# Order of units in the feed-forward layers of a two-block transformer kernel: both down units ahead of P4, T4 later, T1 later in one layer

## Chip, core and metric

One NeuronCore of a Trainium2 chip runs the whole kernel in one launch. The metric is the device time of one execution in microseconds (us). TensorE multiplies; ScalarE (ACT) and VectorE (DVE) prepare its operands and take its results; GpSimd (POOL) issues accumulating transfers and computes small statistics; SyncE (SP) issues most loads. All data is float32.

## What is computed

The input is 256 tokens of width 1024. A first block applies a forgetting attention with a pooling branch, a cross attention over a memory and a gated feed-forward layer; a second block has two layers with two gated feed-forward layers each, a short gated convolution in the first and a differential attention in the second. So there are five feed-forward layers, and most of the time is theirs. In short form:

```
gu  = rmsnorm(h) @ w_gate_up            # 1024 -> 2 * 2816
act = silu(gu[:, :2816]) * gu[:, 2816:]
h   = h + act @ w_down                  # 2816 -> 1024
```

In the second block the result is normalised and halved before it is added. The change touches only the order of work inside these five layers.

## The kernel before

**Precision.** A float32 matrix X is used as two float32r parts, hi = round(X) by ScalarE and lo = X - hi by VectorE, and each product is three matmuls (hi by lo, lo by hi, hi by hi; lines 2115 to 2117, for the down projection 2571 to 2573). So for every unit of weights, a 128x2048 tile, ScalarE writes `w_hi` (line 769 from a loaded tile `w_raw`, line 1084 from a block or a sum of blocks) and then VectorE writes `w_lo` (line 1366), and TensorE waits for `w_lo`. There are three slots for the parts; ScalarE may write unit u once TensorE has used unit u-3 in the order of the list `FFN_OPS`.

**The products.** The up projection of a layer f (0 to 4; "first" to "fifth") has 11 column groups of 256. Groups N0, N1 and N2 are multiplied plainly. The other eight form four pairs p = 0 to 3 (in the texts the number in brackets, P5(1), is the pair). A pair is a 2x2 problem of weight blocks (B11, B12, B21, B22) and token halves, done with seven products P1 to P7 in place of eight. P1, P2 and P3 use B11, B21 and B22; the others use sums: T1 (from B11 and B12) for P5, T2 (T1 and B22) for P6, T3 (B12 and B22) for P7 and T4 (T2 and B21) for P4. VectorE computes T1, T2 and T4 with `weight_sum` (line 1385, whole 128x2048 tiles); T1 goes to the tile `KT`, T2 to `VD`, and T4 takes T2's place in `VD`. T3 is made in B12's own place (`Z`) by an accumulating DMA that POOL issues once T1 has been summed (line 601), and for pairs 1 and 2 T4 is made by such a DMA too, once P6's low part is written. So VectorE sums T4 only for pairs 0 and 3. Each product is 12 matmuls of 128x512.

**Results and activations.** ScalarE copies P1, P5 and P6 out of PSUM (`keep`, line 1115), VectorE combines them with later products to C22, C12 and C11 (`result`, lines 1805, 1807, 1809), ScalarE applies silu (`square_gate`, line 1101), VectorE multiplies by the up half (`square_act`, line 1817), TensorE transposes (line 2595), and the transposed activations are split by `act_out` on ScalarE (`act_hi`, line 1121) and VectorE (`act_lo`, line 1823).

**The down projection** has 11 units of 256 rows, 24 matmuls each: D0 and D1 (of N0 and N1), then two for each pair (Da, Db) and DN2. The pair's two units run in the pair behind: Da(p-1) and Db(p-1) with pair p.

**Order.** Every engine executes its own list in order, and the lists are written out by hand; semaphores count the units. `FFN_OPS` gives the order of units, from which the counts of `w_hi`, `w_lo` and `w_used` and the slots follow. In a layer TensorE runs N0, N1, P1(0), P2(0), P5(0), P6(0), P3(0), P7(0), D0, P4(0), D1, and then for each pair P1, P5, P6, the transposes of the activations, P3, P7, Da, P2, P4, Db. The lists of the other engines are the two functions `ffn` of the scalar part (from line 1125) and the vector part (from line 1823), and `ffn` of the sync part for the loads. A load of the next pair's block waits until the block of this pair has been split (`next_block`); B21 of pair 1 also waits until T4(0) has been summed, as that sum reads B21. D1's activations go into the same tiles as D0's, so `act_out(1)` waits until D0 has been used.

Of the kernel before, what the change touches and what calls it, by code (L numbers as in the profile page):

```python
# [53 lines left out]
SQUARES = 4  # L54
GROUPS = SQUARES + 3
FFN_OPS = [("N0a", 0), ("N0b", 0), ("N1a", 0), ("N1b", 0)]
FFN_OPS += [(_n, 0) for _n in ("P1", "P2", "P5", "P6", "P3", "P7")] + [("D0", 0), ("P4", 0), ("D1", 0)]
for _p in range(1, SQUARES):
    FFN_OPS += [("P1", _p), ("P5", _p), ("P6", _p), ("P3", _p), ("P7", _p), ("Da", _p - 1), ("P2", _p), ("P4", _p),
                ("Db", _p - 1)]  # L60
# [97 lines left out]
def build(nc, a, out):  # L158
# [5 lines left out]
    with ctx:  # L164
# [28 lines left out]

        def act_parts(d):

            return (ahi1, alo1) if is_second(d) else (ahi, alo)

        work = sb("work", [P, 4096])
        junk = sb("junk", [P, HALF])
# [205 lines left out]
        def _(sp):  # L405
# [22 lines left out]
            def ffn(f, w_gu, w_dn, first_blocks=None, next_gu=None):  # L428

                u0 = U_FFN[f]  # L430
                gu = w_gu.rearrange("(k p) f -> p k f", p=P)

                def up(name):
                    u = u0 + OP[name, 0]
                    j = {"N0": 0, "N1": 1, "N2": FJ - 1}[name[:2]]
                    k0 = 4 * (name[-1] == "b")
                    r = raw[raw_slot(u)][:, :].rearrange("p (k c) -> p k c", k=4)
                    load(u, [(r[:, :, 0:256], gu[:, k0:k0 + 4, j * 256:j * 256 + 256]),
                             (r[:, :, 256:512], gu[:, k0:k0 + 4, j * 256 + FF:j * 256 + FF + 256])])

                def down(name, p=0):
                    u, d = u0 + OP[name, p], down_block(name, p)
                    rows = w_dn[d * 256:d * 256 + 256, :].rearrange("(k p) f -> p k f", p=P)
                    load(u, [(raw[raw_slot(u)][:, D * k:D * k + D], rows[:, k, :]) for k in range(2)])

                def next_block(name, reader, p):

                    if p + 1 < SQUARES or next_gu is not None:
                        sp.wait_ge(w_lo, u0 + OP[reader, p] - 1)
                        if name == "B21" and p == 0:  # L450
                            sp.wait_ge(t_ok, sums_ready(f, 0, "T4"))
                        block_in(name, (p + 1) % SQUARES, w_gu if p + 1 < SQUARES else next_gu)

                def first_block(name):
                    if first_blocks:
                        block_in(name, 0, w_gu)

                up("N0a")
                up("N0b")
                up("N1a")  # L460
                if f == 4:
                    for w in first_blocks:
                        sp.wait_ge(*w)
                    first_block("B11")
                up("N1b")
                if f in (0, 2):
                    for w in first_blocks:
                        sp.wait_ge(*w)
                    first_block("B11")
                first_block("B12")  # L470
                first_block("B21")
                first_block("B22")
                down("D0")
                down("D1")
                down("Da", 0)
                next_block("B11", "P1", 0)
                next_block("B22", "P3", 0)
                next_block("B21", "P2", 0)
                next_block("B12", "P7", 0)
                down("Db", 0)  # L480
                down("Da", 1)
                for p in range(1, SQUARES):
                    next_block("B11", "P1", p)
                    next_block("B22", "P3", p)
                    next_block("B12", "P7", p)
                    if p == 1:
                        down("Db", 1)
                        next_block("B21", "P2", p)
                        down("Da", 2)
                    elif p == 2:  # L490
                        down("Db", 2)
                        next_block("B21", "P2", p)
                        up("N2a")
                    else:
                        up("N2b")
                        next_block("B21", "P2", p)
                        down("Da", 3)
                        down("Db", 3)
                        down("DN2")
# [253 lines left out]
        def _(act):  # L753
# [297 lines left out]
            def ffn(f, stat, reader, gain, k0=0, kv=False):  # L1051
# [64 lines left out]

                def act_out(d):
                    act.wait_ge(act_t, FJ * f + d + 1)
                    if d == 1:
                        act.wait_ge(w_used, u0 + OP["D0", 0] + 1)  # L1120
                    act.activation(act_parts(d)[0][:, :], act_bank(d)[:, :], ACT.Copy).then_inc(act_hi, 1)

                weights("N1b")
# [15 lines left out]
                keep("P1", 0)  # L1139
                block("P6", 0)  # L1140
                block("P3", 0)
                keep("P5", 0)
                block("P7", 0)
                keep("P6", 0)
                weights("D0")
                block("P4", 0)
                weights("D1")
                act_out(1)
                for p in range(1, SQUARES):
                    block("P1", p)  # L1150
                    square_gate(p - 1, 0)
# [202 lines left out]
        def _(dve):  # L1354
# [405 lines left out]
            def ffn(f, stat, reader, gain, update=lambda t: None, kv=False):  # L1760
# [78 lines left out]
                block("P5", 0)  # L1839
                block("P6", 0)  # L1840
                block("P3", 0)
                weight_sum("T4", f, 0)
                block("P7", 0)
                weights("D0")
                block("P4", 0)
                result("C22", 0)
                weights("D1")
                result("C12", 0)
                weight_sum("T1", f, 1)
                act_out(1)  # L1850
                result("C11", 0)
                for p in range(1, SQUARES):
                    block("P1", p)
                    weight_sum("T2", f, p)
                    block("P5", p)
                    square_act(p - 1, 0)
                    square_act(p - 1, 1)
                    block("P6", p)
                    if p not in ADDED_T4:
                        weight_sum("T4", f, p)  # L1860
                    block("P3", p)
                    block("P7", p)
                    act_out(2 * p)
                    weights("Da", p - 1)
                    act_out(2 * p + 1)
                    block("P2", p)
                    result("C22", p)
                    block("P4", p)
                    result("C12", p)
                    if p + 1 < SQUARES:  # L1870
                        weight_sum("T1", f, p + 1)
                    weights("Db", p - 1)
                    result("C11", p)
                weights("N2a")
                square_act(SQUARES - 1, 0)
                weights("N2b")
# [224 lines left out]
        def _(pe):  # L2101
# [433 lines left out]
            def ffn(f, reader, waits, kv=False, turned=False, nxt=None):  # L2535
# [72 lines left out]
                for p in range(SQUARES):  # L2608
# [18 lines left out]
                        block("P2", p)  # L2627
                    else:
                        down("D0")
                    pe.wait_ge(c_ok, m + 1)  # L2630
                    block("P4", p)
                    if p:
                        down("Db", p - 1)
                    else:
                        down("D1")
                pe.wait_ge(c_ok, 3 * SQUARES * (f + 1))
                up_unit("N2a")
                turn_act(2 * SQUARES, 1 + SQUARES)
# [314 lines left out]
```

## Time and profile before

| | |
|---|---|
| median of 3 runs | 1264.8 us (1263.88 to 1267.02) |
| profiled execution, its own time | 1265.15 us |
| its span, first to last instruction | 1263.4 us |
| mean granted TensorE clock | 0.999 of full speed |
| TensorE busy / weight loads busy | 1249.7 / 1029.2 us |
| VectorE busy | 1042.2 us (82%) |
| ScalarE busy | 804.7 us (64%) |
| GpSimd busy | 197.8 us (16%) |
| read from HBM | 275.24 MB, 219 GB/s over the span |

Busy time is the time in which an engine executes; the share is of the span. TensorE's matmuls are pipelined: a 128x512 matmul is recorded with some 0.39 us, and the next starts 0.23 us after it, so a wait is best read from one start to the next. An instruction's "idle before" is the time in which its engine executed nothing, and the arrow names what ended it. A few matmul records are missing from the trace.

### The profile page before, as it was taken

Reading aid. Unit: us, or ns where it says so; the run is one execution under the profiler, and the core shown is the slowest. Engines: PE = TensorE matmul, PEld = TensorE weight load, DVE = VectorE, ACT = ScalarE, POOL = GpSimd, SP = SyncE. Lnnn points to the kernel's source line nnn. Section 1 sums busy time; section 2 is a strip of 40 time slices with the busy share of each in tenths; the row PEclk is TensorE's granted clock in tenths of the full one; section 3 lists DMA queues with packets and bytes.
Section 4 is the critical chain, followed back from the end, with each engine's and each line's share of the span. In section 5 each row is a group of like instructions: output and inputs, shape, how many; then the busy total and the mean of one; then the engine's idle time right before and its main releaser. Section 6 shows DMA issues by size and latency. Waiting matters only on the chain.

```text
span 1263.4 us, 15541 instructions
## 1 busy us (share of the span) xinstructions
PE 1249.7 (99%) x5897; PEld 1029.2 (81%) x5897; DVE 1042.2 (82%) x1036; ACT 804.7 (64%) x988; POOL 197.8 (16%) x224
## 2 busy tenths in 40 slices
PE   9999999999999999999999999999999999999998
PEld 7888888888888888888878888888888877788886
DVE  6766689999799996767899997999977568899984
ACT  6674576666576664645666664766656467766662
POOL 6142130110001100202301101211001003301100
PEclk9999999999999999999999999999999999999999
DMA  9537498997649955568989978389745535999931
GB/s 335 175 101 229 128 327 251 267 273 250 199 147 253 272 172 187 194 223 213 334 242 247 265 248 260 123 240 274 219 167 179 180 125 170 321 287 263 266 133 44
DMA packets 143003, 277.32 MB, mean 220 GB/s; under 512 B 8993, under 2 KB 39897, under 8 KB 142929
## 3 DMA queue, kind: packets, MB, share of 16 engines
q1 hardware_dynamic: 120192, 229.67, 52.1%
q0 software_dynamic: 22288, 45.54, 19.7%
q8 instruction: 47, 0.77, 0.2%
q10 hardware_dynamic: 448, 1.12, 0.2%
q14 instruction: 28, 0.22, 0.1%
HBM read 275.24 MB, written 1.05 MB: 219 GB/s over the span
## 4 chain that ended last, share of the span: by engine, by line
PE 83%; DVE 8%; DMA 3%; issue 3%; ACT 2%; POOL 0%; SPq 0%; DVEq 0%; POOLq 0%; ACTq 0%
PE B L2115 15%; PE B L2117 15%; PE B L2116 15%; PE B L2571 7%; PE B L2573 7%; PE B L2572 7%; DVE w_lo L1366 5%; PE T L2115 3%; PE T L2117 3%; PE T L2116 3%; DMA Z<-in_ffn_w_gu 2%; DVE VD L1385 1%; ACT w_hi L1084 1%; PE T L2595 1%; DMA VD<-in_ffn_w_gu 1%
## 5 line engine op out<-in xcount | busy, mean ns | idle before, releaser
L1366 DVE TENSOR_TENSOR w_lo<-w_raw,w_hi 128x2048 fp32r<-128x2048 f32 x129 | 296.5, 2300 | 87.3 <-ACT w_hi L769 87.0
L769 ACT ACTIVATE w_hi<-w_raw 128x2048 fp32r<-128x2048 f32 x129 | 247.2, 1919 | 102.2 <-PE B L2573 59.7
L2115 PE MATMUL B<-w_hi,xt_lo 128*128 128x512 f32 x652 | 259.8, 398 | 2.4 <-DVE nat L2029 0.6
L2117 PE MATMUL B<-w_hi,xt_hi 128*128 128x512 f32 x652 | 254.5, 390 | 0.0
L2116 PE MATMUL B<-w_lo,xt_hi 128*128 128x512 f32 x652 | 254.1, 390 | 0.0
L2571 PE MATMUL B<-w_hi,act_lo 128*128 128x512 f32 x440 | 172.8, 393 | 0.8 <-DVE w_lo L1366 0.6
L2573 PE MATMUL B<-w_hi,act_hi 128*128 128x512 f32 x440 | 171.5, 390 | 0.0
L2572 PE MATMUL B<-w_lo,act_hi 128*128 128x512 f32 x440 | 171.3, 389 | 0.0
L2115 PEld LDWEIGHTS B<-w_hi,xt_lo 128*128 128x128 f32 x652 | 122.5, 188 | 31.5 <-issue 4.4
L2117 PEld LDWEIGHTS B<-w_hi,xt_hi 128*128 128x128 f32 x652 | 122.4, 188 | 26.1
L2116 PEld LDWEIGHTS B<-w_lo,xt_hi 128*128 128x128 f32 x652 | 122.6, 188 | 23.3
L2115 PE MATMUL B<-w_hi,mem_T_lo 128*128 128x512 f32 x296 | 118.6, 401 | 0.9 <-DVE w_lo L1366 0.9
L2117 PE MATMUL B<-w_hi,mem_T_hi 128*128 128x512 f32 x296 | 115.6, 391 | 0.0
L2116 PE MATMUL B<-w_lo,mem_T_hi 128*128 128x512 f32 x296 | 115.4, 390 | 0.0
L1084 ACT ACTIVATE w_hi<-VD 128x2048 fp32r<-128x2048 f32 x40 | 76.8, 1920 | 55.9 <-PE B L2573 34.8
L2571 PEld LDWEIGHTS B<-w_hi,act_lo 128*128 128x128 f32 x440 | 82.6, 188 | 19.7 <-DVE w_lo L1366 2.0
L2573 PEld LDWEIGHTS B<-w_hi,act_hi 128*128 128x128 f32 x440 | 82.6, 188 | 17.4
L2572 PEld LDWEIGHTS B<-w_lo,act_hi 128*128 128x128 f32 x440 | 82.6, 188 | 16.6
L1366 DVE TENSOR_TENSOR w_lo<-Z,w_hi 128x2048 fp32r<-128x2048 f32 x40 | 91.4, 2286 | 4.3 <-ACT w_hi L1084 4.3
L1366 DVE TENSOR_TENSOR w_lo<-VD,w_hi 128x2048 fp32r<-128x2048 f32 x40 | 91.5, 2287 | 2.2 <-ACT w_hi L1084 2.1
L601 POOL DMA_DIRECT2D Z<-in_ffn_w_gu x32 | 39.0, 1449 | 331.9 <-DVE KT L1385 331.9
L1084 ACT ACTIVATE w_hi<-Z 128x2048 fp32r<-128x2048 f32 x40 | 76.5, 1913 | 9.3 <-PE B L2117 5.1
(331 smaller groups left out, 2115.9 us busy)
## 6 DMA issues: line engine op xcount, KB each, us to landing
w_raw<-in_ffn_w_down SPq DMA_DIRECT2D x88, 512.0 KB, 5.8
Z<-in_ffn_w_gu SPq DMA_DIRECT2D x64, 512.0 KB, 8.2
w_raw<-in_ffn_w_gu SPq DMA_DIRECT2D x48, 512.0 KB, 5.3
nat<-in_ffn_w_gu SPq DMA_DIRECT2D x32, 512.0 KB, 7.9
QT<-in_ffn_w_gu SPq DMA_DIRECT2D x32, 512.0 KB, 7.0
Z<-in_ffn_w_gu POOLq DMA_DIRECT2D x32, 512.0 KB, 9.1
w_raw<-in_conv_w_in SPq DMA_DIRECT2D x24, 512.0 KB, 4.8
w_raw<-in_w_down SPq DMA_DIRECT2D x22, 512.0 KB, 6.6
```

The costliest lines, as they stand in the source:

```text
L601: pool.dma_start(r[:, i:i + 2, :], gu[:, 4 + i:6 + i, col:col + HALF], accum_op=ALU.add)\
L769: act.activation(whi[home(u)][:, :], raw[slot][:, :], ACT.Copy).then_inc(w_hi, 1)
L1084: act.activation(whi[home(u)][:, :], (WB[src] if src in WB else WT[src]), ACT.Copy).then_inc(w_hi, 1)
L1366: dve.tensor_tensor(wlo[home(u)][:, :], src, whi[home(u)][:, :].bitcast(F32), ALU.subtract).then_inc(w_lo, 1)
L1385: dve.tensor_tensor(WT[name], src, WB[block_name], ALU.add).then_inc(t_ok, 1)
L2115: pe.matmul(bank[:, :], lo[:, k, x], whi[s][:, c], start=first, stop=False, skip_group_check=more)
L2116: pe.matmul(bank[:, :], hi[:, k, x], wlo[s][:, c], start=False, stop=False, skip_group_check=more)
L2117: return pe.matmul(bank[:, :], hi[:, k, x], whi[s][:, c], start=False, stop=last, skip_group_check=more)
L2571: pe.matmul(o, lo[:, x], whi[slot][:, c], start=d == 0 and k == 0, stop=False)
L2572: pe.matmul(o, hi[:, x], wlo[slot][:, c], start=False, stop=False)
L2573: ins = pe.matmul(o, hi[:, x], whi[slot][:, c], start=False, stop=d == FJ - 1 and k == 1)
L2595: ins = pe.transpose(act_bank(d)[:, (2 * k + t) * P:(2 * k + t) * P + P], actn[:, t, c0 + k * P:c0 + k * P + P], ident[:, :])
```

## The change

1. *First pair of every layer.* The order of units becomes P7, D0, D1, P4 in place of P7, D0, P4, D1, on TensorE and in `FFN_OPS`. D1's activations get the second pair of tiles (`ahi1`, `alo1`), so `act_out(1)` no longer waits for D0; it moves to just behind P3's unit on ScalarE and on VectorE. ScalarE splits D1 ahead of P4. On VectorE T4(0) moves from ahead of P7's low part to behind D0's, P4's low part to behind C12, and C11 comes ahead of T1(1). SP issues the load of B12 ahead of that of B21.
2. *Fourth pair of every layer.* On VectorE T4(3) moves from ahead of P3's low part to behind the second `act_out` of the pair, ahead of P2's.
3. *Third layer only (f == 2), pairs 1 and 2.* On VectorE T1 of the next pair moves from ahead of Db's low part to behind Db's low part and C11.

```diff
-FFN_OPS += [(_n, 0) for _n in ("P1", "P2", "P5", "P6", "P3", "P7")] + [("D0", 0), ("P4", 0), ("D1", 0)]
+FFN_OPS += [(_n, 0) for _n in ("P1", "P2", "P5", "P6", "P3", "P7", "D0", "D1", "P4")]
...
         def act_parts(d):
-            return (ahi1, alo1) if is_second(d) else (ahi, alo)
+            return (ahi1, alo1) if d == 1 or is_second(d) else (ahi, alo)
...
                 next_block("B11", "P1", 0)
                 next_block("B22", "P3", 0)
+                next_block("B12", "P7", 0)
                 next_block("B21", "P2", 0)
-                next_block("B12", "P7", 0)
...
                 def act_out(d):
                     act.wait_ge(act_t, FJ * f + d + 1)
-                    if d == 1:
-                        act.wait_ge(w_used, u0 + OP["D0", 0] + 1)
...
                 block("P3", 0)
+                act_out(1)
                 keep("P5", 0)
                 block("P7", 0)
                 keep("P6", 0)
                 weights("D0")
+                weights("D1")
                 block("P4", 0)
-                weights("D1")
-                act_out(1)
...
                 block("P3", 0)
-                weight_sum("T4", f, 0)
+                act_out(1)
                 block("P7", 0)
                 weights("D0")
-                block("P4", 0)
+                weight_sum("T4", f, 0)
                 result("C22", 0)
                 weights("D1")
                 result("C12", 0)
+                block("P4", 0)
+                result("C11", 0)
                 weight_sum("T1", f, 1)
-                act_out(1)
-                result("C11", 0)
                 for p in range(1, SQUARES):
...
                     block("P6", p)
-                    if p not in ADDED_T4:
-                        weight_sum("T4", f, p)
                     block("P3", p)
                     block("P7", p)
                     act_out(2 * p)
                     weights("Da", p - 1)
                     act_out(2 * p + 1)
+                    if p not in ADDED_T4:
+                        weight_sum("T4", f, p)
                     block("P2", p)
                     result("C22", p)
                     block("P4", p)
                     result("C12", p)
-                    if p + 1 < SQUARES:
+                    if p + 1 < SQUARES and f != 2:
                         weight_sum("T1", f, p + 1)
                     weights("Db", p - 1)
                     result("C11", p)
+                    if p + 1 < SQUARES and f == 2:
+                        weight_sum("T1", f, p + 1)
...
                     else:
                         down("D0")
+                        down("D1")
                     pe.wait_ge(c_ok, m + 1)
                     block("P4", p)
                     if p:
                         down("Db", p - 1)
-                    else:
-                        down("D1")
```

## Rows read from the trace of the kernel before

**Rows 1.** The page: the span, and busy us, share and instructions of TensorE.
```profile
span 1263.4 us, 15541 instructions
...
PE 1249.7 (99%) x5897; PEld 1029.2 (81%) x5897; DVE 1042.2 (82%) x1036; ACT 804.7 (64%) x988; POOL 197.8 (16%) x224
```

**Rows 2.** Busy time by stretch: stretch, us long, busy us by engine, clock, DMA share, GB/s.
```profile
core 0: us, PE busy (x) PEld busy (x) DVE busy (x) ACT busy (x) POOL busy (x), PEclk, DMA share, GB/s
...
206.00:214.00 8.00, 8.00 (x37) 6.57 (x36) 7.92 (x7) 3.99 (x5) 2.07 (x2) 1.00 0.89 324
```

**Rows 3.** Timeline of TensorE, first layer, last matmul of P3(0) and first of P7(0).
```profile
200.85 0.39 PE L2117 MATMUL B<-w_hi,mem_T_hi 128*128 128x512 f32 x1
201.52 0.47 PE L2115 MATMUL T<-w_hi,mem_T_lo 128*128 128x512 f32 x1 [0.28 <-DVE w_lo L1366]
```

**Rows 4.** List of waits, whole span: us in total, times, longest.
```profile
PE T L2115 <- DVE w_lo L1366: 1.3, 5, 0.3
...
PE B L2571 <- DVE act_lo L1823: 0.2, 1, 0.2
...
DVE KT L1385 <- DMA Z<-in_ffn_w_gu: 1.8, 4, 0.6
```

**Rows 5.** Timeline of VectorE, first layer: T4(0), P7, act_lo(1), P5(1), P6(1).
```profile
196.88 2.29 DVE L1385 TENSOR_TENSOR VD<-VD,QT 128x2048 f32<-128x2048 f32 x1
199.09 2.28 DVE L1366 TENSOR_TENSOR w_lo<-Z,w_hi 128x2048 fp32r<-128x2048 f32 x1
...
211.55 0.68 DVE L1823 TENSOR_TENSOR act_lo<-T,act_hi 128x512 fp32r<-128x512 f32 x1
...
217.15 2.29 DVE L1366 TENSOR_TENSOR w_lo<-KT,w_hi 128x2048 fp32r<-128x2048 f32 x1
...
220.68 2.29 DVE L1366 TENSOR_TENSOR w_lo<-VD,w_hi 128x2048 fp32r<-128x2048 f32 x1
```

**Rows 6.** Timeline of ScalarE, first layer: copy of P5(0), high parts of P7(0), D0.
```profile
195.84 0.60 ACT L1115 ACTIVATE work<-B 128x512 f32<-128x512 f32 x1 [1.20 <-PE B L2117]
196.33 1.91 ACT L1084 ACTIVATE w_hi<-Z 128x2048 fp32r<-128x2048 f32 x1
...
199.05 1.91 ACT L769 ACTIVATE w_hi<-w_raw 128x2048 fp32r<-128x2048 f32 x1
```

**Rows 7.** Timeline of TensorE, first layer: first matmuls of P1(1) and P5(1).
```profile
217.94 0.39 PE L2115 MATMUL B<-w_hi,xt_lo 128*128 128x512 f32 x1
...
220.66 0.39 PE L2115 MATMUL B<-w_hi,mem_T_lo 128*128 128x512 f32 x1
```

**Rows 8.** Timeline of TensorE: transposes to P3(2), P3(3) of layer 1, P3(3) of layer 2.
```profile
256.92 0.60 PE L2595 MATMUL T<-ident,work 128*128 128x128 f32 x4
...
257.71 0.48 PE L2115 MATMUL T<-w_hi,mem_T_lo 128*128 128x512 f32 x1
...
287.73 0.60 PE L2595 MATMUL T<-ident,work 128*128 128x128 f32 x4
...
288.70 0.47 PE L2115 MATMUL B<-w_hi,mem_T_lo 128*128 128x512 f32 x1
...
464.47 0.60 PE L2595 MATMUL T<-ident,work 128*128 128x128 f32 x4
...
465.94 0.47 PE L2115 MATMUL B<-w_hi,mem_T_lo 128*128 128x512 f32 x1 [0.44 <-DVE w_lo L1366]
```

**Rows 9.** Timeline of TensorE, third layer: last matmul of P4(2), first of Db(1).
```profile
721.88 0.39 PE L2117 MATMUL B<-w_hi,xt_hi 128*128 128x512 f32 x1
722.85 0.50 PE L2571 MATMUL B<-w_hi,act_lo 128*128 128x512 f32 x1 [0.58 <-DVE w_lo L1366]
```

**Rows 10.** Timeline of VectorE, third layer: T1(2).
```profile
686.62 2.29 DVE L1385 TENSOR_TENSOR KT<-Z 128x2048 f32<-128x2048 f32 x1 [0.25 <-DMA Z<-in_ffn_w_gu]
```

**Rows 11.** Timeline of ScalarE, third layer: high part of Db(0).
```profile
685.91 1.92 ACT L769 ACTIVATE w_hi<-w_raw 128x2048 fp32r<-128x2048 f32 x1 [2.48 <-PE B L2573]
```

**Rows 12.** Line 601's transfers: T3(1) of the first layer, then T3(2) of the third.
```profile
DMA to landing us min/median/max: 6.0/8.3/10.6
...
DMA to landing us min/median/max: 6.2/9.1/12.0
```

## Prediction

> **What bounds the kernel now.** I read the page first, for the busy share [rows 1]. TensorE is busy 1249.7 of 1263.4 us, so nothing that leaves its work alone can give back much; the change touches no matmul. Then the busy time by stretch: behind the first pair of a layer, from 206 to 214 us, VectorE is busy 7.92 of 8.00 us beside a full TensorE [rows 2]. Two engines are full there, and whoever is late has no room to catch up. So I went to TensorE's timeline and took start to start, since recorded ends overlap the next start. A 128x512 matmul follows the last after 0.23 us; every larger step between two products is a stall. The first matmul of P7 in the first layer starts 201.52 after 200.85, 0.67 us, so 0.44 lost, and it takes 0.47 instead of 0.39, as the first one behind a wait does: 0.08 more [rows 3]. What releases it is VectorE's low part of P7. In the list of waits it stands five times, once a layer [rows 4]: 1.3 us of idle time, plus the 0.16 of overlapped matmul tail each, is 2.1 us. That is what the first edit aims at.
>
> **The first pair, taken away.** VectorE starts the next instruction 0.08 us before the recorded end of the last, so 2048 columns cost 2.20 and 512 columns 0.60 (the 0.68 of act_lo less 0.08) [rows 5]. T4 now sits between P3's low part and P7's. Taken out, P7's low part no longer waits for VectorE but for ScalarE's high part, 196.33+1.91=198.24 [rows 6], and ends at 200.55 instead of 201.37. TensorE could use it at 201.08. The five waits go: 0.44+0.08 in this layer, about 0.5 in each. D1 can follow D0, since its activations are split before P5's copy, in ScalarE's 1.20 us of idle time at 195.84 [rows 6]; with that D1's wait for act_lo in the third layer (0.2 idle and 0.16 of tail [rows 4]) goes too.
>
> **The first pair, given back.** VectorE is the queue to follow. Between the start of T4 (196.88) and that of P5(1)'s low part (217.15) lie 20.27 us [rows 5]: eight large instructions and four small ones (8x2.20+4x0.60=20.0) and 0.27 idle. The change keeps all twelve but opens two gaps that T4 filled: act_lo(1) is done at 197.48 and P7's high part at 198.24, so 0.78 idle; then P7's low part is done at 200.47 and D0's high part only at 199.05+1.91=200.96, so 0.51 idle. ScalarE can't be earlier: its slots come free by TensorE's P5 and P6. P5(1)'s low part therefore starts at 196.88+20.0+1.3=218.2, ends at 220.47, and is usable 0.15 later (201.37 against 201.52 [rows 3, 5]) at 220.6. TensorE, 0.5 earlier than its 220.66 [rows 7], asks at 220.2: it waits 0.45. P6(1)'s low part follows 3.53 us after P5's (217.15 to 220.68, one low part and two gated products [rows 5]), but P5 keeps TensorE only 2.72+0.08 (217.94 to 220.66 for such a block [rows 7]): it waits a further 0.73. Once P5 waits, P6 always waits 0.73. With 0.08 for the first matmul after each, the first layer loses 0.45+0.73+0.16-0.52, some 0.85 us net. Fourth and fifth have the same pattern: 0.85 each. In the second a small wait before a later D unit shrinks by the same shift: 0.65. In the third D1's 0.4 and its 0.08 go too: 0.35, if VectorE follows as in the first (it now waits 0.6 us there for B12, one of four such waits [rows 4], and no longer does). Sum of the first edit: **+3.55**.
>
> The queues it is moved past: T1(1) is 2.2 us later, so POOL's accumulating transfer T3(1) is too (10.6 us from its second issue, 0.7 behind the first, to landing in this layer, so about 225.5 [rows 12]); P7(1)'s high part waits for that to 225.6, low part done 229.8, TensorE asks at 230.5. No cost, 0.6 us in hand. On SP the load of B12 goes ahead by 0.8, and B21 waits for T4, 205.5 instead of 199.3, with Db(0) and Da(1) queued behind it 3 us and none late: they are read after 232. P4's own low part is done at 211.1, asked at 214.7. Free, as long as the loads take what they take now.
>
> **T4(3) behind P3.** In the fourth pair TensorE issues eight transposes and then P3. Where nothing is late that takes 257.71-256.92=0.79 us; with T4(3) ahead 0.97 in the first layer and 1.47 in the second [rows 8]. So 0.18 in three layers and 0.68 in two (the third is like the second): **-1.9**. Its new place is in front of P2, whose low part has 3 us in hand. Free.
>
> **T1 behind D's second unit, third layer.** There Db(1) waits 722.85-721.88-0.23=0.74 [rows 9], and 0.1 goes at its first matmul and 0.1 at Db(0): 0.95 gained. The cost: VectorE is free at 686.37, 0.25 ahead of T1's 686.62 [rows 10], and now has Db(0)'s low part next, whose high part ends at 685.91+1.92=687.83 [rows 11]. It idles 1.49 where it idled 0.25, T1's slot, so P1, T2, P5 and P6 come 1.24 later. By the arithmetic above: P5(2) waits about 0.37 and P6(2) 0.73, and again in the next pair. T1(2) itself ends 4 us later (692.9), and POOL's transfer queues behind it: its second half lands 12.0 us after its issue [rows 12], at 705.9; P7(2)'s high and low parts take 1.92+2.30 and it is usable at 710.3, asked at 709.4: 0.84, and Da behind it 0.47 and 0.38. Sum 3.9, with 0.08 at six first matmuls 4.4, less 0.95: +3.4. The unknown is the landing, as the transfer now meets other loads. No row shows it there. If it lands 0.5 us sooner the edit costs 2.4 and 1 us sooner 1.6; 1 us later, 5.4. The span of its kind is 10.6 to 12.0 [rows 12]; I take the upper end less a little: **+3.0**.
>
> **Sum.** 3.55-1.9+3.0=+4.65 us. The profiled execution took 1265.15 us (span 1263.4), 0.35 above the median of 1264.8; the sum gives 1269.8 on the first and 1269.45 on the second. I say 1269.5.
>
> **A rule to weigh.** The rows show where TensorE has its gaps: at P7, at P3 and at the D units [rows 3, 4, 8, 9], 5.8 us in all. The Trainium skill, "Perfetto Trace Analysis", section Identifying Performance Opportunities, says to take the engine with the highest occupancy, find its gaps and make what ends them come sooner. By that rule alone this change is a gain, and it is the first rival; the sum above differs because VectorE, which ends those gaps, is itself full [rows 2].
>
> **Rivals.**
> *All the waits go and none come* (7%). VectorE would have to reach P5(1) 0.45 and P6(1) 1.2 us sooner than my sum; its place is the pair of gaps of 0.78 and 0.51. For it: P5(1) is now ready at 219.44, 1.2 us ahead of its use [rows 5, 7], more than either gap. Against: the two gaps together are 1.3 and TensorE asks 0.5 sooner. All that is removed is 2.1+0.4 (first matmuls)+0.4+1.9+1.0=5.8: 1259.0. It decides where the two gaps together fall under 0.86 us for P5(1) (219.59 is usable now with 0.27 idle, 220.18 is asked) and under 0.1 for P6(1).
> *Only the first pairs lose* (24%). POOL's transfer in the third layer lands a microsecond or more sooner, or the loads leave VectorE ready earlier, and the third edit costs 0 to 1.5: 3.55-1.9+0.7=+2.3, 1267. For it: the load that T1 waited for is long in by then.
> *Transfers collide* (13%). B21, Db(0), Da(1) now follow one another from 205.5 and the additions start later, in stretches where the DMA engines are busy 0.89 of the time [rows 2]; each microsecond later puts waits at P7 and P4. With landings 1 us later the second layer loses 1.4 and the third 2 more: +8, 1273. The Trainium skill, "DMA: Bandwidth & Descriptors", section Issuing engines are not separate DMA queues, says that transfers of every issuing engine interleave on the same 16 engines; by it POOL's additions slow whenever SP's bunch up, and this rival is where it would show.
> That the change moves nothing has no room: the orders are written by hand and TensorE's follows them.
>
> **Numbers.** Forecast 56% (+2.8 to +7), the rivals 24, 13 and 7. A measurement of this kernel can tell 0.3% (3.8 us) from no change. Faster by more: only nearly all of the first rival, 0.03. Within: the second rival, the rest of the first and the low end of the forecast, 0.33. Slower: 0.64. The range leaves out the first rival and the far end of the third: 1265 to 1273.5.
>
> **What would show it.** Right: in each layer TensorE has no wait at P7(0), and waits near 0.4 at P5(1) and 0.7 at P6(1) for VectorE's low part; VectorE idle 0.8 and 0.5 ahead of P7's and D0's low parts; transposes to P3(3) in 0.8; in the third layer no wait at Db, but at P5, P6 of both later pairs and at P7(2) behind POOL's transfer. Wrong: no wait at P5(1), or the third layer not longer than the first.

## The result, and the profile after

The changed kernel takes 1276.96 us (1276.61 to 1278.67, 4 runs), the kernel before 1264.86 beside it: 1.0093 times as long, 95% interval 1.0081 to 1.0105. That is 12.1 us more where 4.65 were forecast, and beyond the range of 1265 to 1273.5. The profiled execution took 1278.67 us. Its page, to be set against [rows 1] (the third line is the chain of work that ended last, where TensorE's share was 83%, VectorE's 8 and the DMA's 3):

```profile
span 1276.8 us, 15536 instructions
PE 1254.8 (98%) x5897; PEld 1027.9 (81%) x5897; DVE 1042.7 (82%) x1036; ACT 805.1 (63%) x988; POOL 198.4 (16%) x224
PE 66%; DVE 12%; DMA 9%; issue 7%; ACT 4%; POOL 1%; DVEq 0%; SPq 0%; POOLq 0%; ACTq 0%
```

The work is the same on every engine. TensorE's busy time is 5 us up, mostly because the recorded tail of a matmul ahead of a wait is no longer overlapped. What is new is DMA on the chain: 9%. The list of waits, TensorE's alone, of after (us in total, times, longest):

```profile
PE B L2115 <- DVE w_lo L1364: 5.9, 13, 0.6
PE B L2571 <- DVE w_lo L1364: 4.3, 9, 1.2
PE T L2115 <- DVE w_lo L1364: 1.1, 2, 0.6
```

The five waits at P7(0) [rows 4] are gone. Of the fifteen waits at line 2115, one, at 51 us, has nothing to do with the change and is in both kernels; fourteen at the square products stand where before had seven (the five of 1.3 us at P7(0) and two at P3(3)). Ahead of the down units (line 2571) there are nine where it had one of 0.6 us. Where they lie, TensorE's timeline of the first layer tells:

```profile
201.24 0.39 PE L2117 MATMUL B<-w_hi,mem_T_hi 128*128 128x512 f32 x1
201.46 0.39 PE L2115 MATMUL T<-w_hi,mem_T_lo 128*128 128x512 f32 x1
...
220.28 0.39 PE L2117 MATMUL B<-w_hi,xt_hi 128*128 128x512 f32 x1
221.02 0.47 PE L2115 MATMUL B<-w_hi,mem_T_lo 128*128 128x512 f32 x1 [0.36 <-DVE w_lo L1364]
...
223.64 0.39 PE L2117 MATMUL B<-w_hi,mem_T_hi 128*128 128x512 f32 x1
224.55 0.47 PE L2115 MATMUL B<-w_hi,mem_T_lo 128*128 128x512 f32 x1 [0.52 <-DVE w_lo L1364]
...
244.38 0.39 PE L2117 MATMUL B<-w_hi,xt_hi 128*128 128x512 f32 x1
245.43 0.50 PE L2571 MATMUL B<-w_hi,act_lo 128*128 128x512 f32 x1 [0.67 <-DVE w_lo L1364]
```

P7(0) follows P3(0) in 0.22 us, where [rows 3] had 0.67. P5(1) waits 221.02-220.28-0.23=0.51 and P6(1) 0.68: forecast were 0.45 and 0.73. Then Db(0) waits 0.82, and that was not in the forecast. By layer, Db(0) waits 0.83, 1.37, 0, 0.51 and 1.10 us, Db(1) 0.36, 0.53, 0, 0, 0.33, and Da(0) 0.2 to 0.35 in the last four. The way back from the third wait, Db(0)'s, is in VectorE's timeline (answers to [rows 5]):

```profile
198.66 2.29 DVE L1364 TENSOR_TENSOR w_lo<-Z,w_hi 128x2048 fp32r<-128x2048 f32 x1 [0.71 <-ACT w_hi L1084]
201.38 2.29 DVE L1364 TENSOR_TENSOR w_lo<-w_raw,w_hi 128x2048 fp32r<-128x2048 f32 x1 [0.42 <-ACT w_hi L769]
...
222.12 2.28 DVE L1364 TENSOR_TENSOR w_lo<-VD,w_hi 128x2048 fp32r<-128x2048 f32 x1
224.32 2.28 DVE L1364 TENSOR_TENSOR w_lo<-nat,w_hi 128x2048 fp32r<-128x2048 f32 x1
...
238.09 2.29 DVE L1364 TENSOR_TENSOR w_lo<-VD,w_hi 128x2048 fp32r<-128x2048 f32 x1 [1.14 <-ACT w_hi L1084]
...
243.09 2.29 DVE L1364 TENSOR_TENSOR w_lo<-w_raw,w_hi 128x2048 fp32r<-128x2048 f32 x1
```

The two gaps ahead of P7's and D0's low parts, 0.71 and 0.42, are the forecast 0.78 and 0.51. Db(0)'s low part ends at 245.38; it is late because P4(1)'s low part could only start at 238.09. ScalarE's timeline (answers to [rows 6]) says why. P4(1)'s high part waits for a transfer:

```profile
236.14 1.92 ACT L1084 ACTIVATE w_hi<-VD 128x2048 fp32r<-128x2048 f32 x1 [2.99 <-DMA VD<-in_w_gate_up]
```

So the chain to Db(0) begins at POOL's accumulating transfer of T4(1). POOL's issue and SP's next one, of before and then of after:

```profile
223.27 2.38 POOL L601 DMA_DIRECT2D VD<-in_w_gate_up  x2 [8.96 <-DVE w_lo L1366]
225.68 0.96 SPq L426 DMA_DIRECT2D nat<-in_w_gate_up  x2
DMA to landing us min/median/max: 6.2/7.8/9.4
```

```profile
224.70 2.38 POOL L601 DMA_DIRECT2D VD<-in_w_gate_up  x2 [7.76 <-DVE w_lo L1364]
226.63 1.14 SPq L426 DMA_DIRECT2D nat<-in_w_gate_up  x2
DMA to landing us min/median/max: 6.0/8.3/10.7
```

The addition goes out in two halves (x2), 0.7 us between their starts; the landing rows give the shorter and the longer time of the two, each from its own issue. The first lands in about 6 us in both (the minimum). The second lands in 9.4 before and 10.7 after; in the second and third layers it is over 2 us later. And SP's load of B22 (the tile `nat`) comes 2.41 us behind POOL's first issue before, 1.93 after. That offset became the question of the experiments.

How little room there was stands in the trace of before, in rows that the prediction did not use: ScalarE's P4(1) high part, VectorE's low part of Db(0) and TensorE's Db(0) in the first layer, then the last two in the second.

```profile
233.39 1.92 ACT L1084 ACTIVATE w_hi<-VD 128x2048 fp32r<-128x2048 f32 x1 [1.50 <-DMA VD<-in_w_gate_up]
...
240.35 2.28 DVE L1366 TENSOR_TENSOR w_lo<-w_raw,w_hi 128x2048 fp32r<-128x2048 f32 x1
...
243.31 0.39 PE L2571 MATMUL B<-w_hi,act_lo 128*128 128x512 f32 x1
...
417.29 2.28 DVE L1366 TENSOR_TENSOR w_lo<-w_raw,w_hi 128x2048 fp32r<-128x2048 f32 x1
...
419.63 0.50 PE L2571 MATMUL B<-w_hi,act_lo 128*128 128x512 f32 x1
```

Db(0) had 0.68 us in hand in the first layer (242.63 to 243.31), 0.06 in the second and third, 0.72 and 0.73 in the last two.

### The profile page after: what moved, and what is told of

It is laid out like the page before. It is cut to its first block, busy times and chain, and to the rows that moved or that the text cites. A ratio compares the mean times of both kernels' runs of the same rounds, so it can differ in the third digit from the quotient of the medians.

```text
span 1276.8 us, 15536 instructions
## 1 busy us (share of the span) xinstructions
PE 1254.8 (98%) x5897; PEld 1027.9 (81%) x5897; DVE 1042.7 (82%) x1036; ACT 805.1 (63%) x988; POOL 198.4 (16%) x224
## 3 DMA queue, kind: packets, MB, share of 16 engines
HBM read 275.24 MB, written 1.05 MB: 216 GB/s over the span
## 4 chain that ended last, share of the span: by engine, by line
PE 66%; DVE 12%; DMA 9%; issue 7%; ACT 4%; POOL 1%; DVEq 0%; SPq 0%; POOLq 0%; ACTq 0%
PE B L2115 13%; PE B L2117 13%; PE B L2116 13%; DVE w_lo L1364 7%; PE B L2571 5%; PE B L2573 5%; PE B L2572 5%; DMA VD<-in_ffn_w_gu 4%; DMA Z<-in_ffn_w_gu 3%; PE T L2117 2%; PE T L2115 2%; PE T L2116 2%; DVE KT L1383 2%; DMA VD<-in_w_gate_up 2%; ACT w_hi L769 2%
## 5 line engine op out<-in xcount | busy, mean ns | idle before, releaser
L1084 ACT ACTIVATE w_hi<-Z 128x2048 fp32r<-128x2048 f32 x40 | 76.6, 1915 | 31.9 <-DMA Z<-in_ffn_w_gu 11.2
```

What stands on the lines that cost most here:

```text
L1084: act.activation(whi[home(u)][:, :], (WB[src] if src in WB else WT[src]), ACT.Copy).then_inc(w_hi, 1)
```

## The experiments

Medians, with the ratio to the kernel before and its 95% interval. Each edit is against the kernel before unless it says otherwise.

**Each part alone.** The first edit is the hunks of the diff that stand under number 1 of the change; at its core:

```diff
-FFN_OPS += [(_n, 0) for _n in ("P1", "P2", "P5", "P6", "P3", "P7")] + [("D0", 0), ("P4", 0), ("D1", 0)]
+FFN_OPS += [(_n, 0) for _n in ("P1", "P2", "P5", "P6", "P3", "P7", "D0", "D1", "P4")]
```

> The first edit alone (D1 ahead of P4, T4(0) and T1(1) later, B12 ahead of B21), T4(3) and the third layer's T1 as before. Theory 'late addition': T1(1) late makes POOL's transfer T3(1) land some 3 to 7 us later, T4(1) right behind it, and Db(0) waits; this edit holds nearly all of the loss, +12 to +14 us, with TensorE waits near 0.5 at P5(1), 0.7 at P6(1) and 0.5 to 1.4 at Db(0) in each layer. Rival 'sum as predicted': the edit alone is +3.5 and the rest of the loss comes from the other two edits. P3(3)'s step from its transposes stays at 1.0 to 1.5 us, or Db(1) takes the wait.

Measured 1278.02, ratio 1.0106 (1.0092 to 1.0120), some 13.5 us where 3.55 stood in the sum. That is 10 us too little for this part, more than the 7.5 by which the whole sum was short; the parts do not simply add up (below).

The second edit alone:

```diff
                     block("P6", p)
-                    if p not in ADDED_T4:
-                        weight_sum("T4", f, p)
...
                     act_out(2 * p + 1)
+                    if p not in ADDED_T4:
+                        weight_sum("T4", f, p)
```

> Only T4(3) moved from ahead of P3's low part to ahead of P2's. By the predicted sum it gives back 0.18 us in three layers and 0.68 in two, -1.9 us in all (0.15%), and the step from the transposes to P3(3) is 0.8 us in every layer. Rival: T4(3) in its new place makes P2(3) or Db(2) wait, 0 or more.

Measured 1262.48, ratio 0.9984 (0.9975 to 0.9992). TensorE's timeline of the first layer, the transposes of the fourth pair (the first four of eight) and P3(3):

```profile
287.60 0.60 PE L2595 MATMUL T<-ident,work 128*128 128x128 f32 x4
...
288.39 0.48 PE L2115 MATMUL B<-w_hi,mem_T_lo 128*128 128x512 f32 x1
```

0.79 from transposes to P3(3) as forecast, 0.97 in [rows 8], and in the second layer 464.70-463.91=0.79 too.

The third edit alone:

```diff
-                    if p + 1 < SQUARES:
+                    if p + 1 < SQUARES and f != 2:
                         weight_sum("T1", f, p + 1)
                     weights("Db", p - 1)
                     result("C11", p)
+                    if p + 1 < SQUARES and f == 2:
+                        weight_sum("T1", f, p + 1)
```

> Only the third layer's T1(2) and T1(3) moved behind Db's low part and C11. Predicted sum: no wait at Db(0) and Db(1), waits at P5 and P6 of pairs 2 and 3 of 0.4 and 0.7, P7(2) 0 to 0.9 by when POOL's transfer lands; +3.0 us (1.6 to 5.4). Rival 'fill': the load T1 waited for is long in and the third layer is not longer, -0.5 to +1.

Measured 1268.17, ratio 1.0030 (1.0019 to 1.0040): +4.0, forecast +3.0. Its waits in the third layer are at P5(2) and P6(2), where they were forecast (timeline of TensorE), and again at P5(3) and P6(3), 0.89 and 0.71:

```profile
698.43 0.39 PE L2119 MATMUL B<-w_hi,xt_hi 128*128 128x512 f32 x1
699.11 0.47 PE L2117 MATMUL T<-w_hi,mem_T_lo 128*128 128x512 f32 x1 [0.29 <-DVE w_lo L1366]
...
701.70 0.39 PE L2119 MATMUL T<-w_hi,mem_T_hi 128*128 128x512 f32 x1
702.64 0.47 PE L2117 MATMUL B<-w_hi,mem_T_lo 128*128 128x512 f32 x1 [0.55 <-DVE w_lo L1366]
```

The first and second edits together:

> First and second edit, the third layer's T1 as before. If the third edit costs what it costs alone (+3), this is 3 us faster than the changed kernel, near 1274. If in the changed kernel VectorE is late there anyway and Db(0) of the third layer would wait as in the other layers, the third edit is worth about nothing in company and this is 1276 to 1277, with Db(0) waiting 0.8 to 1.6 in the third layer too.

Measured 1275.17, ratio 1.0088 (1.0073 to 1.0104). So in company the third edit costs less than alone, 1.8 us by the medians and 0.6 by the ratios: without it Db(0) of the third layer waits 1.8 us behind T4(1), with it not at all, since VectorE then sums T1(2), 2.2 us, only behind Db(0)'s low part.

**Which piece of the first edit.** First theory: the additions are late because T1(1) ends 2.2 us later. The first edit, with T1(1) behind D1's low part, and a wait so that T2(1) is not written before P4's low part is done:

```diff
+                weight_sum("T1", f, 1)
                 result("C12", 0)
                 block("P4", 0)
                 result("C11", 0)
-                weight_sum("T1", f, 1)
...
+                    if p == 1:
+                        dve.wait_ge(w_lo, u0 + OP["P4", 0] - 1)
                     weight_sum("T2", f, p)
```

> The first edit with one thing changed: VectorE sums T1(1) right behind D1's low part, 3.4 us sooner than in the edit and 1 us sooner than in the kernel before. Theory 'late addition' (T3(1) is issued late and T4(1) cannot land before some 10 us after T3(1) has): T3(1) lands near 222, T4(1) near 235, Db(0) waits 0 to 0.3 us; P5(1) and P6(1) still wait 0.5 and 0.7. So +3 to +6 us against before, 8 to 10 less than the first edit. Rival 'loads' (B21, Db(0) and Da(1) loaded later are what makes the additions slow or Db late): these loads are as in the edit, so Db(0) waits as it did and the time stays near 1278.

Measured 1277.62, ratio 1.0096 (1.0082 to 1.0110). The theory fell: T3(1) landed at 223.3 in place of 226.0 in the first layer, and Db(0) still waited 1.73 us, behind a T4(1) of 12.3 us.

Next, D1 ahead of P4 as in the change, but VectorE's T4(0) ahead of P7's low part and SP's order as before:

```diff
                 block("P3", 0)
                 weight_sum("T4", f, 0)
                 block("P7", 0)
                 weights("D0")
-                block("P4", 0)
+                act_out(1)
                 result("C22", 0)
                 weights("D1")
                 result("C12", 0)
-                weight_sum("T1", f, 1)
-                act_out(1)
+                block("P4", 0)
                 result("C11", 0)
+                weight_sum("T1", f, 1)
```

> D1 ahead of P4 as in the first edit, but T4(0) stays ahead of P7's low part and SP's loads keep their order; T1(1) stays behind C11, 1.4 us later than before. P7(0) waits its 0.44 again. VectorE has no gaps of 0.8 and 0.5, so P5(1) and P6(1) wait 0 to 0.1. Theory 'late addition' splits here: if an addition slows because it is issued late, T3(1) lands some 12 us after its issue and Db(0) waits 0.5 to 1.5 (+3 to +7 us in all); if it slows because of the loads beside it, T3(1) lands after 10 us, T4(1) is not held, Db(0) waits under 0.3 and the time is -1 to +2.

Measured 1267.41, ratio 1.0016 (1.0007 to 1.0026). T3(1) is as slow as in the changed kernel (11.4 to 12.5 us), yet T4(1) takes 10.0 to 10.5 in all layers and Db(0) waits 0.12 at most. So a slow T4(1) does not come from a slow T3(1) ahead of it. The same, with T1(1) behind D1's low part and the same added wait:

```diff
                 weights("D1")
+                weight_sum("T1", f, 1)
                 result("C12", 0)
                 block("P4", 0)
                 result("C11", 0)
-                weight_sum("T1", f, 1)
```

> D1 ahead of P4 on TensorE and ScalarE, T4(0) ahead of P7's low part and T1(1) right behind D1's low part (where it waits for B12's load near 207 to 208.5). If the two late sums are the whole harm of the first edit, this is the kernel before less D1's wait in the third layer: -0.5 us, between -1.5 and +1. If putting D1 ahead of P4 itself costs (slots, P5(1)'s high part behind D1, gates behind P4), +2 or more.

Measured 1269.54, ratio 1.0036 (1.0022 to 1.0050), a miss. This run split by layer. In the first, fourth and fifth T4(1) took 9.9 to 10.2 us and Db(0) did not wait; in the second and third it took 12.3 and 12.5, and Db(0) waited 1.69 and 1.89. One kernel, one order, two durations. The rows of its second layer, POOL's issue and SP's:

```profile
401.62 2.43 POOL L601 DMA_DIRECT2D VD<-in_ffn_w_gu  x2 [11.04 <-DVE w_lo L1364]
403.55 1.19 SPq L426 DMA_DIRECT2D nat<-in_ffn_w_gu  x2
```

1.93 us between the issues in these two layers, 2.12 in the other three. That gave the theory that the next runs test: a load that SP issues before POOL has got its second half out goes in ahead of that half, and it lands some 2 us later.

**The theory, forwards.** The changed kernel, with SP's load of B22 held back until ScalarE has written P7's high part:

```diff
                         sp.wait_ge(w_lo, u0 + OP[reader, p] - 1)
...
+                        if name == "B22" and p in (1, 2):
+                            sp.wait_ge(w_hi, u0 + OP["P7", p] - 1)
```

> The changed kernel, with one thing added: SP issues the loads of B22 for pairs 2 and 3 only when ScalarE has written P7's high part, about 1.3 us later than now. Theory (a load that SP issues before POOL has issued the second half of its accumulating transfer gets in ahead of that half): in every layer T4(1) lands 9.9 to 10.5 us after its first issue instead of 11.4 to 12.7, the waits at Db(0) (0.83, 1.37, 0.51 and 1.10 us over the usual step of 0.23) go, and 4 to 5 us come back: 1272.5. The waits at P5(1), P6(1) and Da(0) stay. Rival (the transfer is slow because it starts late, among more loads): it lands as late as before and the time stays at 1277.

Measured 1271.98, ratio 1.0051 (1.0037 to 1.0065): 5 us back, by delaying a load. T4(1) took 9.1 to 10.1 us in every layer and no Db waits. POOL's and SP's issues of the first layer and the landing, and TensorE at Db(0):

```profile
224.98 2.38 POOL L603 DMA_DIRECT2D VD<-in_w_gate_up  x2 [7.76 <-DVE w_lo L1366]
228.17 0.99 SPq L426 DMA_DIRECT2D nat<-in_w_gate_up  x2
DMA to landing us min/median/max: 6.0/7.6/9.3
```

```profile
244.66 0.39 PE L2119 MATMUL B<-w_hi,xt_hi 128*128 128x512 f32 x1
244.88 0.39 PE L2573 MATMUL B<-w_hi,act_lo 128*128 128x512 f32 x1
```

The load comes 3.19 us behind now, the second half lands in 9.3, and Db(0) follows P4(1) in 0.22.

**And T3's too.** On top of it, SP's load of B11 behind T2:

```diff
+                        if name == "B11" and p:
+                            sp.wait_ge(t_ok, sums_ready(f, p, "T2"))
```

> As the run with B22 later, and SP also issues the load of B11 for the next pair only behind T2 of this one, 2.2 us later than now, so that it follows both halves of T3's transfer. Theory: T3(1) to T3(3) land about 10 us after their issue instead of 11.1 to 12.5, P7(1)'s high part no longer waits for T3(1) (idle 1.33 us in the first layer), the waits at Da(0) of 0.2 to 0.34 go in four layers, and 1 to 2 us more come back: 1271. Rival: landings and time do not move.

Measured 1276.34, ratio 1.0085 (1.0072 to 1.0099): the time missed by 5 us, the landings in part. T3(1) landed 8.4 to 9.0 us after its issue, where it took 11.3 to 12.1 in the run before, and the waits at Da(0) went. But P7(1)'s high part, no longer held by T3(1), now ended so early that waiting for it delayed SP no more. Timeline of POOL and SP, first layer:

```profile
224.36 2.38 POOL L605 DMA_DIRECT2D VD<-in_w_gate_up  x2 [7.76 <-DVE w_lo L1368]
226.28 1.16 SPq L426 DMA_DIRECT2D nat<-in_w_gate_up  x2
```

1.93 us again in all five layers (here by the rounded rows 1.92); T4(1) took 11.6 to 12.4 again and Db(0) waited 0.97 to 1.84 in four of them. It is a second, unplanned test of the offset, and it speaks for it.

**The theory, backwards.** The kernel before, with POOL's transfer a little later, so that SP's load falls inside its two issues (`tick` is a new tile of 8 columns that nothing reads):

```diff
                     pool.wait_ge(w_lo, U_FFN[f] + OP["P6", p] - 1)
+                    if p == 1:
+                        pool.wait_ge(w_hi, U_FFN[f] + OP["P3", p] - 1)
+                        pool.memset(tick[:, :], 0.0)
```

> The kernel before, with the one thing reversed: POOL issues T4(1)'s transfer some 0.4 to 0.5 us later, behind ScalarE's high part of P3(1) and a memset of 8 columns, so that SP's load of B22 comes 1.9 to 2.0 us behind the first issue instead of 2.4. Theory of the load that gets in: the transfer takes 12 us or more instead of 10.1, lands 2.4 us later, and Db(0), whose low part is ready only 0.05 to 0.75 us ahead of TensorE in the kernel before, waits 1.8 us in the first, fourth and fifth layers and 2.4 in the second and third: 1264.9+10=1275. Rival (lateness alone): it lands 0.45 later, Db(0) waits 0.4 in two layers, 1266.

Measured 1275.74, ratio 1.0085 (1.0069 to 1.0100): +10.6, forecast +10. Waits of TensorE, and POOL, SP and TensorE of the first layer:

```profile
PE B L2575 <- DVE w_lo L1370: 8.5, 6, 1.9
```

```profile
223.94 0.10 POOL L603 MEMSET tick<- 128x8 f32 x1 [9.13 <-ACT w_hi L1088]
224.39 2.39 POOL L605 DMA_DIRECT2D VD<-in_w_gate_up  x2 [0.35 <-issue]
226.16 1.32 SPq L427 DMA_DIRECT2D nat<-in_w_gate_up  x2
...
244.98 0.50 PE L2575 MATMUL B<-w_hi,act_lo 128*128 128x512 f32 x1 [1.01 <-DVE w_lo L1370]
```

The offset is 1.77, T4(1) takes 11.3 to 12.5 us and Db(0) waits 1.2 to 2.1 in all layers. The issue itself is 0.65 us later than before (224.39 against 223.27, in an execution that is 0.47 behind at P7(0)). Lateness of 0.65 alone would have put next to nothing on the three layers with 0.68 to 0.73 in hand, and 0.6 on the other two.

All T4(1) transfers, five layers in each of fourteen kernels, sorted by the time from POOL's first issue to SP's next load:

| SP's load behind POOL's first issue | transfers | first issue to landing |
|---|---|---|
| 1.77 to 1.93 us | 32 | 11.27 to 13.20 us |
| 2.12 to 3.93 us | 38 | 9.15 to 10.48 us in 36, 11.3 in 2 |

The two exceptions are in the second layer of the kernels below, at 2.42 and 2.85.

**The queues in the trace.** The packets that start on each DMA queue show what the two transfers do to each other. In the first layer of before queue q0 carries 1.05 MB from POOL's first issue (223.27) to 234, the size of the addition, so q0 is POOL's and q1 has SP's loads. The microsecond from 5.5 to 6.5 us behind POOL's first issue, in before (228.77 to 229.77) and then in after (230.20 to 231.20), as packets, MB, share of the 16 DMA engines:

```profile
q0 software_dynamic: 67, 0.13, 74.0%
q1 hardware_dynamic: 31, 0.06, 23.7%
```

```profile
q1 hardware_dynamic: 182, 0.37, 100.4%
q0 software_dynamic: 3, 0.00, 0.5%
```

Before, the addition goes on beside the load. After, it stops between its halves while SP's load has the engines. In that microsecond q0 starts 0 to 4 KB in all 32 transfers of the first row of the table and 94 to 194 KB in all 38 of the second. In the two exceptions it did not stop: 98% of the transfer had started by 9.2 us, as in the other 36, and the last packets followed one by one, 0.25 us apart.

T4(1) is not alone. Of the other additions in two halves that POOL issues from 200 us on (T3 and the other T4), 313 have a first half that lands within 7 us (51 do not, and are left out). With SP's next load 1.93 us behind or less, all 180 took 11.05 us or more; with it 2.08 or more behind, 116 of 133 took under 10.5 (the others, most of them in the second and third layers, up to 11.7). The trace of before had this already: there T3(1) has the next load 3.1 us behind and takes 10.0 to 10.2 in four layers (11.3 in the first), T3(2) and T3(3) have it 1.93 behind and take 11.2 to 13.6.

**The parts that pay.** The second edit, with D1's activations in their own tiles and ScalarE's `act_out(1)` behind P3, so that the third layer's wait for act_lo goes; the units in the order of before:

```diff
-            return (ahi1, alo1) if is_second(d) else (ahi, alo)
+            return (ahi1, alo1) if d == 1 or is_second(d) else (ahi, alo)
...
                 result("C22", 0)
+                if f == 2:
+                    act_out(1)
                 weights("D1")
                 result("C12", 0)
                 weight_sum("T1", f, 1)
-                act_out(1)
+                if f != 2:
+                    act_out(1)
```

> The kernel before with T4(3) behind P3 (measured -1.7 us) and D1's activations in their own tiles, split ahead of P5's copy on ScalarE; on VectorE act_out(1) stands ahead of D1's low part in the third layer alone. The third layer's D1 no longer waits (0.45 us). Expected -2.1 us against before (-1.3 to -3), the fastest so far. If it is only -1.7 or less, the time saved at D1 is taken by the next wait of that layer, at Db.

Measured 1262.58, ratio 0.9977 (0.9968 to 0.9987): the fastest by ratio (the second edit alone has the lower median, 1262.48, beside other runs of before), ahead of both kernels. The gain of 0.23% is under the 0.3% of the prediction's text, but its interval stays below 1; from the second edit alone it can't be told apart. With both delays of SP's loads on top:

> The kernel with the good parts (T4(3) behind P3, D1's activations in their own tiles), with both delays of SP's loads. Theory: T3(2), T3(3) and both T4 transfers of the second layer land in about 10 us; the two waits at Db in the second layer (0.54 and 0.65) go: 1261.3, 1.2 us under the same kernel without the delays. Rival: 1262.5, as without them.

Measured 1262.84, ratio 0.9981 (0.9973 to 0.9990): no gain, a miss. Its T4(1) were 2.4 us or more ahead of the load already, and the two long transfers of the second layer stayed long (11.3 and 11.6 us, Db waits 0.54 and 1.02), so the offset is not their cause. What made their last packets late stays open.

## Why the prediction was wrong

**What held.** The waits at P7(0) went in all layers. The two gaps, and from them P5(1) and P6(1) by the arithmetic of VectorE's queue: 0.45 and 0.73 forecast, 0.51 and 0.68 to 0.72 measured. T4(3) behind P3: -1.9 forecast, -1.7 measured. T1 in the third layer: +3.0 forecast, +4.0 alone, with waits at the forecast places except P7(2), and one more at P3(3), 740.14 of its timeline, which ScalarE's copy released. Its size came out near by some luck: the 0.84 at P7(2) did not come, and P5(3) waited 0.89 where about 0.4 was forecast.

**What failed** is one step, the queues that the first edit is moved past: "Free, as long as the loads take what they take now." The condition was named, and it did not hold. The step followed T3(1) to P7(1) and stopped. T3(1) landed at 226.0, not 225.5, in the first layer; in the other four it took 11.9 to 12.3 us instead of 10.0 to 10.2, with SP's next load 1.93 us behind its start instead of 3.1, and there Da(0) waits, up to 0.35. T4(1) was not followed in the sum, from its issue by P4(1)'s parts to Db(0). Measured from P7(0), where this execution of after is 0.39 behind that of before apart from the edit (201.24 against 200.85 for the matmul ahead of it), P6(1)'s low part ends 1.05 us later (222.12 against 220.68) and TensorE asks for Db(0) 0.90 later (244.61 against 243.31). So lateness alone takes 0.15 of the slack, which is 0.63 (the 0.68 in hand less the 0.05 from the end of the low part to TensorE's start); the transfer's own 1.3 us more takes the rest and makes the wait: 0.15+1.3-0.63=0.82. In the second layer nothing was in hand; the transfer took 2.6 us longer, and about half of it reached Db(0), a wait of 1.37: VectorE before had waited 0.62 us for another load, ahead of T1(2), and now did not, and TensorE itself lost 0.35 at Da(0). In the third Db(0) does not wait, as T1(2) stands behind it now.

The transfer is longer because SP's load now comes 1.93 us behind POOL's first issue and gets in between the halves: P3(1)'s low part, which that load waits for, follows P6(1)'s back to back, 224.32-222.12=2.20, where VectorE had waited 0.40 for ScalarE and was 2.68 behind. An idle gap of 0.4 us had kept two queues apart. Taking the collision out gives back 5.0 of the 7.5 us by which the sum was short (1276.96 to 1271.98). Of the other 2.5, the five waits at Da units in that run make 1.4 and their first matmuls 0.4; the rest is within the spread of the runs.

**The rivals.** "Transfers collide" was the right one in kind, with 13% and 1273. It was priced as landings 1 us later; T4(1) landed 1.3 to 2.6 us longer after its issue. The two rows of [rows 12] were read as a span, 10.6 to 12.0, and are of two kinds: SP's next load is 3.1 us behind the first transfer, the slowest of the five T3(1) of that trace, and 1.93 behind the second. Its place was wrong too: it set out from B21, Db(0) and Da(1) behind 205.5, and the load that mattered was B22, 20 us later. The Trainium skill, "DMA: Bandwidth & Descriptors", section Issuing engines are not separate DMA queues, was weighed there as the reason why POOL's additions would slow when SP's loads bunch up; the traces agree in kind, as 9.15 to 10.48 against 11.27 to 13.20 us show, and add that here the order of two issues inside half a microsecond decides it (in the microsecond shown above the two did not share the engines, 182 packets against 3), not the amount of traffic: over 222 to 250 us the DMA engines were busy 0.93 of the time before and 0.94 after. By the rule of the first rival, to close TensorE's gaps, the change was a gain; the gaps it aimed at closed, and yet TensorE's steps of over 0.34 us, less 0.23 each, sum to 22.7 us over the span where they summed to 10.9.

**What is not shown.** The packets show that POOL's queue stops while SP's load runs; they do not show why. The limit lies between 1.93 and 2.08 us in these runs (T3(0) of two layers, at 2.08 to 2.09, takes 9.3 to 9.8), so it is not the end of POOL's issue, which takes 2.4 us; what sets it is open. So is what makes 19 of the 171 additions with a later load take 10.5 to 11.7 us.

## What to carry to other kernels

When an edit makes an engine late by more than its slack, follow every transfer that its instructions release to the last reader, and look up how much that reader has in hand (here 0.06 to 0.73 us), not only the first one behind it. Compare the issue times of different queues too: a small idle gap can be what keeps one queue's load behind another's, and a load that nobody is short of can be delayed at no cost to bring a needed one in sooner. Then try each part alone: one of three parts paid, and the sum hid it.

## What was not expected of the hardware

An accumulating transfer of 1 MB in two halves, 2.38 us of issue on POOL, lands in about 10 us when the next load of SP is issued 2.1 us or more behind its start and in about 12 when it is issued 1.8 to 1.9 behind, with the exceptions told above; the first half lands in 6 us either way, and the second half's packets start about a microsecond later. With the next load 4.2 us behind, T3(1) took 8.4 to 9.0.

In the run with POOL's transfer held back, TensorE waited 2.06 us at Db(0) of the third layer, and 1.5 us behind the wait's end its matmuls followed one another in 0.43 us instead of 0.23 for seven steps, as at the lower level of 1.2 GHz. The busy time by stretch shows the granted clock (the column behind POOL's) at 0.72 over six microseconds, which mixes both levels, and at 1.00 before and after them:

```profile
core 0: us, PE busy (x) PEld busy (x) DVE busy (x) ACT busy (x) POOL busy (x), PEclk, DMA share, GB/s
690.00:697.00 7.00, 5.73 (x25) 4.25 (x24) 6.72 (x4) 4.09 (x3) 1.33 (x2) 1.00 0.71 273
697.00:703.00 6.00, 5.37 (x16) 4.26 (x17) 6.00 (x5) 3.10 (x3) 1.08 (x1) 0.72 0.94 195
703.00:710.00 7.00, 7.00 (x32) 5.81 (x31) 5.40 (x4) 4.11 (x3) 0.36 (x1) 1.00 0.91 283
```

It cost about 1.4 us (7 times 0.2) in the profiled execution, part of that run's +10.6.
